# Attention's end in a two-block kernel: four outputs of the out projection in two parts

## The chip, the cores and the metric

One core of one Trainium2 chip runs the whole kernel. The metric is device time in microseconds of the core, and a kernel is judged by the median of its runs. The engines are TensorE (PE), VectorE (DVE), ScalarE (ACT), GpSimd (POOL) and SyncE (SP); each runs its own instructions in program order and waits on semaphores. PEld in the profile is TensorE's weight load, which overlaps its matmuls.

## What is computed

The input is 512 tokens of width 1024 in float32. A first block has two layers (stick-breaking attention, then an HGRN2 mixer, each followed by a squared-ReLU MLP), a second block two more. The change lies at the end of the attention of the first layer and at the start of the MLP behind it:

```python
def first_block(x, ...):
    for layer in range(DEPTH):
        h = rmsnorm(x, norm_gains[layer, 0])
        if layer % N_MIXERS == 0:
            x = x + stick_breaking_mixer(h, ...)   # ends with: return o @ w_o
        else:
            x = x + hgrn2_mixer(h, ...)
        h = rmsnorm(x, norm_gains[layer, 1])
        x = x + squared_relu_mlp(h, mlp_w1[layer], mlp_w2[layer])
    return x

def stick_breaking_attention(q, k, v):   # for each block of 128 queries
    log_stay = where(causal, log_sigmoid(-z), 0.0)
    log_between = cumsum(log_stay, axis=3, reverse=True) - log_stay
    weights = where(causal, exp(log_sigmoid(z) + log_between), 0.0)
    out = weights @ v
```

There are 16 heads of width 64. The out projection is 512 x 1024 by 1024 x 1024.

## The kernel before

**Layout.** Everything is kept transposed: x, h and the attention's output are [128 partitions, 8 blocks, 512 tokens], a block being 128 of the 1024 features. A product with a weight matrix is made of output tiles of 128 features. One output needs 8 weight blocks of 128 x 128 (k = 0 to 7), each against a 512 token block of the right input.

**Three matmuls a block.** For accuracy each operand is split into a high part (the value rounded to fp32r) and a low part (the rest). `gemm` (L234) issues, for the weight blocks it is given, first all high x high (L243), then high weights x low input (L247), then low weights x high input (L250). It waits for the high part of the weight tile at its head, for the low part only before L250. The last matmul of a tile raises `tile_used`.

**The weight stream.** Weights come as tiles of 8 blocks (512 KB) in one stream in the order of use. SyncE loads tile t into a ring of 4 raw buffers once the low part of tile t-3 is made (L1926). ScalarE makes the high part, `split_hi` (L215), into one of two buffers, which it may do only once tile t-2 is used. GpSimd makes the low part in four instructions of two blocks each, `split_lo` (L223), also into two buffers. In this stretch the tiles are called T (= T_ATT_O) to T+7 for the out projection, T+8 and on for the MLP. The outputs go by turns into two PSUM banks, `ps_g[0]` and `ps_g[1]`.

**The attention's pipeline.** Eight head pairs run through `pipelined` (L722), which in each step works on three of them in program order: g makes Q, K and V (three weight tiles), a computes scores and stick-breaking weights, b ends. The scores of a pair come in four units, for the query blocks 3, 2, 0, 1 in that order. A unit goes: scores on TensorE (L506); absolute value, exponential and logarithm on ScalarE (L580, L585, L590); add, two scans and subtract on VectorE (L656, L662, L664); exponential on ScalarE (L595); transposes on TensorE (L514); copies of the two heads by ScalarE (L600) and VectorE (L669). Two score units share their banks with the transposed weights, so a unit's scores wait for the copies of one before it. After the four units comes P.V (L524, 16 matmuls with 64-column weights into `ps_o`), then the high part by ScalarE (L605, `ohi`) and the low part by VectorE (L674, `olo`): these are block k of the out projection's input, k being the pair. V is turned by four transposes (L443) and a copy (L449).

**The drain.** In the step in which no g is left (a = pair 7, b = pair 6), `att_pe` gives TensorE parts of the out projection in the places of the QKV tiles: `out(0, 0, 3)`, `out(0, 3, 6)`, `out(1, 0, 3)`, `out(1, 3, 6)`, then block 6 of both. Their input blocks 0 to 6 are ready by then. The next step ends pair 7: its last transposes, P.V, ohi, olo. `out_begun_pe` then adds block 7 to outputs 0 and 1 and computes outputs 2 to 7 whole, 24 matmuls each:

```python
for d in range(2):
    gemm(pe, At(T + d), T + d, rhs, kts, False, True, ready, None, True)
for d in range(2, KT):
    gemm(pe, At(T + d), T + d, rhs, ALL, True, True, None, (x_ready, R + d - 1))
```

**Behind each output.** VectorE adds it to the residual x (`resid_dve`, L363, semaphore `x_ready`), ScalarE makes the high part of the next input h (L292) and the square of x (L382), VectorE the low part (L302) and the sum of squares (L374). `split_hi` of the tile after next stands ahead of each output's work on ScalarE (`out_act`).

**The MLP's start.** `ffn_pe` computes the first MLP tile T+8 in two halves of four blocks; between them stands `norm_pe` (L327), one product of a matrix of ones with the sum of squares (two passes), which needs all eight sums. The MLP's own norm factor is applied only at its end; ScalarE makes it from this sum ahead of the first relu (L309, L312; L857). A second MLP behind the other mixer runs the same code.

Of the kernel before, what the change touches and what calls it, by code (L numbers as in the profile page):

```python
# [8 lines left out]
P = 128  # L9
# [103 lines left out]
def build_program(nc, stream, ada_w, x_in, vecs_in, mats_in, lvmask_in, wgk_in, y_out):  # L113
    with ExitStack() as ctx:
# [119 lines left out]
        def gemm(pe, t, o, rhs, kts, first, last, waits=None, free=None, used=None, banks=None):  # L234
# [17 lines left out]
            if kts[-1][1] == KT - 1 if used is None else used:  # L252
                ins.then_inc(tile_used, 1)

        def h_rhs(k):
# [274 lines left out]


        def att_pe(pe, g, a, b):
            t = g.map(3, T_ATT) if g else None
            drain = a and not g

            def free(i):
                return (au_ready, t.of(1, i - 1)) if t.rep + i >= 2 else None

            def out(d, k0, k1):
                gemm(pe, At(T_ATT_O + d), T_ATT_O + d, a_rhs, ALL[k0:k1], k0 == 0, False,  # L540
                     lambda e, k, term: e.wait_ge(olo_ready, k + 1), (au_ready, 3 * PAIRS - 1 + d) if k0 == 0 else None)
# [24 lines left out]
            if g: gemm(pe, t + 2, t.rep, h_rhs, H1, True, False, None, free(2))  # L566
            if drain: out(0, 6, 7)
            if g: att_unit.pe_stat(pe, g.map(2, 1))
            if a: att_z(pe, a, 1)
            if drain: out(1, 6, 7)  # L570
            if a: att_wt(pe, a, 0)
            if g: gemm(pe, t + 2, t.rep, h_rhs, H2, False, True)
# [33 lines left out]

        def att_act(act, g, a, b):
            t = g.map(3, T_ATT) if g else None
            if a:
# [4 lines left out]
            if g: split_hi(act, t + 1)  # L614
            elif a: split_hi(act, At(T_ATT_O + 1))
            if b: att_first_act(act, b, 1)
# [76 lines left out]

        def att_dve(dve, g, a, b):
            if a: att_u_dve(dve, a, 2, vT_b)
            if b: att_second_dve(dve, b, 1)
# [18 lines left out]
        def att_pool(pool, g, a, b):  # L715
            t = g.map(3, T_ATT) if g else None
            if g:
                for i in range(3):
                    split_lo(pool, t + (i + 1))
            elif a: split_lo(pool, At(T_ATT_O + 1))  # L720

# [91 lines left out]
        def ffn_pe(pe, m, T, n, R, Q):  # L813
            for half in range(2):
                U = (2 * m + half) * FH
                for quarter in (2 * half, 2 * half + 1):
                    for j in quarter_loop(pe, m, quarter):
                        for k in range(4):
                            t, u = ffn_tile(m, T, quarter, j, k)
                            if quarter == 0 and j == 0 and k == 0:  # L820
                                pe.wait_ge(x_ready, R - 1)
                                gemm(pe, t, k, h_rhs, H1, True, False, h_waits(n), (relu_done, before(u)))
                                norm_pe(pe, n)
                                gemm(pe, t, k, h_rhs, H2, False, True, h_waits(n))
                            else:
# [1119 lines left out]
        def _(pe):  # L1945
            pipelined(pe, att_pe, PAIRS)
            out_begun_pe(pe, T_ATT_O, 0, lambda e, k, term: e.wait_ge(olo_ready, PAIRS), ALL[KT - 1:], a_rhs)
            ffn_pe(pe, 0, T_MLP0, 1, KT, 2 * KT)
# [10 lines left out]
        def _(act):  # L1959
# [9 lines left out]
            pipelined(act, att_act, PAIRS)  # L1969
            out_act(act, T_ATT_O, 0, KT, nxt=(1, GAIN[1]))  # L1970
            ffn_act(act, 0, T_MLP0, 1, KT, 2 * KT, (2, GAIN[2]))
# [10 lines left out]
        def _(dve):  # L1982
# [39 lines left out]
            pipelined(dve, att_dve, PAIRS)  # L2022
            out_dve(dve, T_ATT_O, 0, KT, nxt=(1, GAIN[1]))
            ffn_dve(dve, 0, T_MLP0, 1, KT, 2 * KT, (2, GAIN[2]))
# [14 lines left out]
        def _(pool):  # L2039
            split_lo(pool, At(0))  # L2040
            pipelined(pool, att_pool, PAIRS)
            out_pool(pool, T_ATT_O)
            ffn_pool(pool, 0, T_MLP0, 1, KT, 2 * KT)
# [8 lines left out]
def lay_out(np, a):  # L2052
# [6 lines left out]
    def ffn(w1, w2):  # L2059
        out = []  # L2060
        for half in range(2):
# [4 lines left out]
        return np.concatenate(out)  # L2066

    full = [P * d for d in range(KT)]
    stream = [tiles(a["sb_w_qkv"][0], [D_MODEL * m + P * p for p in range(PAIRS) for m in range(3)]),
              tiles(a["sb_w_o"][0], full), ffn(a["mlp_w1"][0], a["mlp_w2"][0]),  # L2070
              tiles(a["hg_w_in"][0], [D_MODEL * m + P * h for h in range(HG_HEADS) for m in (1, 2, 0, 3)]),
# [55 lines left out]
```

## Time and profile before

| | us |
|---|---|
| median of three runs (1850.20 to 1850.63) | 1850.24 |
| profiled execution, its own time | 1851.17 |
| its span, first to last instruction | 1849.4 |
| TensorE busy in the span | 1800.9 (97%) |
| last QKV tile's end to the first full out projection tile | 222.19 to 258.25 |
| from there to the first MLP tile T+8 | 258.25 to 291.24 |
| start of the second MLP tile, T+9 | 298.07 |

Times in the views are microseconds from the start of the span, "us" a duration; "mean ns" is that of one instruction. A row of the timeline may merge several instructions of one kind (x8), and the bracket is the time the engine sat idle before it and what ended that. Ends of matmuls are modelled and overlap the next start by 0.2 to 0.3 us, so distances between starts are the better measure of TensorE's work. PEclk is the granted clock, 1.00 for 2.4 GHz and 0.50 for 1.2 GHz.

### The profile page before, as it was taken

To read this page: it belongs to the slowest core of one execution; us is meant where nothing else is said; L and a number is where in the kernel's file an instruction comes from. 1 tells how busy PE (TensorE), PEld (TensorE's weight loads), DVE (VectorE), ACT (ScalarE), POOL (GpSimd) and SP (SyncE) were. 2 spreads that over 40 slices of the span, in tenths; PEclk is the share of its full clock that TensorE was granted. 3 is DMA by queue.
4 is the path that set the end of the run, shared out by engine and by line. 5 is a ranking of instruction groups with operands and counts; after the bars stand their busy time and mean duration, and the time that the engine had idled before them with its cause. 6 is when DMAs were issued, how large, how long until landed. Compare 5 with 4: busy or idle time off the path is not lost.

```text
span 1849.4 us, 25940 instructions
## 1 busy us (share of the span) xinstructions
PE 1800.9 (97%) x8406; PEld 1415.8 (77%) x8406; DVE 1029.0 (56%) x1659; ACT 891.5 (48%) x1384; POOL 890.1 (48%) x1072
## 2 busy tenths in 40 slices
PE   7999989999999999999899999999999999999999
PEld 5666658888888788888688888888776777776777
DVE  5677655621563377878666413643535565636562
ACT  6767744421333356666443312432456565455562
POOL 3343336755675533444217655766533336533343
PEclk9999989999999999999899999999999999999999
DMA  4111114432453222221145423533221222222212
GB/s 161 67 58 57 57 55 158 164 114 91 159 170 102 91 80 69 69 68 57 35 129 179 137 91 125 180 117 101 80 80 58 69 69 80 80 75 63 79 58 91
DMA packets 49659, 176.82 MB, mean 96 GB/s; under 512 B 5648, under 2 KB 5776, under 8 KB 49568
## 3 DMA queue, kind: packets, MB, share of 16 engines
q1 hardware_dynamic: 42368, 149.44, 25.5%
q10 hardware_dynamic: 7200, 26.22, 4.1%
q8 instruction: 50, 0.82, 0.2%
q14 instruction: 41, 0.34, 0.1%
HBM read 173.54 MB, written 2.10 MB: 95 GB/s over the span
## 4 chain that ended last, share of the span: by engine, by line
PE 81%; DVE 9%; ACT 4%; issue 3%; POOL 1%; DMA 0%; DVEq 0%; ACTq 0%; SPq 0%; POOLq 0%
PE ps_g L243 17%; PE ps_g L250 16%; PE ps_g L247 16%; PE ps_zt L243 6%; PE ps_zt L247 6%; PE ps_zt L250 6%; PE ps_s L1574 1%; PE ps_zt L514 1%; PE ps_zt L1623 1%; PE ps_zt L1001 1%; PE ps_o L524 1%; PE ps_o L1030 1%; PE ps_s L415 1%; PE ps_o L1638 1%; POOL w_lo L223 1%
## 5 line engine op out<-in xcount | busy, mean ns | idle before, releaser
L223 POOL TENSOR_TENSOR w_lo<-raw,w_hi 128x256 fp32r<-128x256 f32 x936 | 779.8, 863 | 791.9 <-ACT w_hi L215 790.6
L215 ACT ACTIVATE w_hi<-raw 128x1024 fp32r<-128x1024 f32 x274 | 288.8, 1054 | 376.7 <-PE ps_zt L250 247.0
L243 PE MATMUL ps_g<-h_hi,w_hi 128*128 128x512 f32 x1240 | 346.5, 409 | 10.1 <-ACT h_hi L292 8.6
L247 PE MATMUL ps_g<-h_lo,w_hi 128*128 128x512 f32 x1240 | 323.9, 391 | 1.0 <-DVE h_lo L302 1.0
L250 PE MATMUL ps_g<-h_hi,w_lo 128*128 128x512 f32 x1240 | 322.5, 390 | 0.7 <-POOL w_lo L223 0.4
L243 PEld LDWEIGHTS ps_g<-h_hi,w_hi 128*128 128x128 f32 x1240 | 224.4, 189 | 76.4 <-issue 23.6
L247 PEld LDWEIGHTS ps_g<-h_lo,w_hi 128*128 128x128 f32 x1240 | 233.3, 188 | 53.4 <-DVE h_lo L302 2.3
L250 PEld LDWEIGHTS ps_g<-h_hi,w_lo 128*128 128x128 f32 x1240 | 233.0, 188 | 51.2 <-POOL w_lo L223 1.2
L359 DVE TENSOR_TENSOR scr<-ps_zt,scr 128x512 f32<-128x512 f32 x32 | 22.1, 692 | 255.0 <-PE ps_zt L250 255.0
L857 ACT ACTIVATE scr<-ps_g 128x512 f32<-128x512 f32 x64 | 38.3, 599 | 193.2 <-PE ps_g L250 193.2
L243 PE MATMUL ps_zt<-a_hi,w_hi 128*128 128x512 f32 x512 | 128.6, 393 | 0.0
L247 PE MATMUL ps_zt<-a_lo,w_hi 128*128 128x512 f32 x512 | 127.4, 391 | 0.0
L250 PE MATMUL ps_zt<-a_hi,w_lo 128*128 128x512 f32 x512 | 126.9, 390 | 0.0
L243 PE MATMUL ps_g<-a_hi,w_hi 128*128 128x512 f32 x408 | 117.4, 412 | 6.7 <-DVE a_lo L1279 3.1
L243 PEld LDWEIGHTS ps_zt<-a_hi,w_hi 128*128 128x128 f32 x512 | 96.1, 188 | 21.8
L247 PEld LDWEIGHTS ps_zt<-a_lo,w_hi 128*128 128x128 f32 x512 | 96.1, 188 | 21.1
L250 PEld LDWEIGHTS ps_zt<-a_hi,w_lo 128*128 128x128 f32 x512 | 96.1, 188 | 20.6
L247 PE MATMUL ps_g<-a_lo,w_hi 128*128 128x512 f32 x408 | 108.7, 391 | 0.0
L250 PE MATMUL ps_g<-a_hi,w_lo 128*128 128x512 f32 x408 | 108.6, 391 | 0.0
L808 DVE TENSOR_TENSOR scr<-scr 128x1024 f32<-128x1024 f32 x48 | 69.9, 1456 | 59.4 <-DMA scr<-ada_weights 58.9
L243 PEld LDWEIGHTS ps_g<-a_hi,w_hi 128*128 128x128 f32 x408 | 73.5, 190 | 33.1 <-issue 15.0
L1318 POOL TENSOR_TENSOR scr<-scr 128x256 f32<-128x256 f32 x56 | 47.6, 849 | 92.7 <-DVE scr L1201 47.6
(211 smaller groups left out, 2402.4 us busy)
## 6 DMA issues: line engine op xcount, KB each, us to landing
raw<-weights SPq DMA_DIRECT2D x274, 512.0 KB, 3.5
scr<-ada_weights ACTq DMA_DIRECT2D x48, 512.0 KB, 4.2
x<-x_tiles SPq DMA_DIRECT2D x8, 256.0 KB, 5.7
y<-x SPq DMA_DIRECT2D x8, 256.0 KB, 3.2
scr<-csil_dram ACTq DMA_DIRECT2D x2, 512.0 KB, 5.7
lvmask<-level_masks SPq DMA_DIRECT2D x1, 960.0 KB, 9.3
mats<-squares SPq DMA_DIRECT2D x1, 448.0 KB, 7.0
vecs<-vectors SPq DMA_DIRECT2D x1, 95.5 KB, 2.0
```

What stands on the lines that cost most here:

```text
L215: nc.scalar.activation(w_hi[:, t.rep % 2], raw[:, raw_slot(t)], ACT.Copy).then_inc(whi_ready, 1)
L223: ins = nc.gpsimd.tensor_tensor(w_lo[:, t.rep % 2, ks], raw[:, raw_slot(t), ks], w_hi[:, t.rep % 2, ks].bitcast(F32), ALU.subtract)
L243: nc.tensor.matmul(bank[:], w_hi[:, t.rep % 2, kk], rhs(k)[0], start=(first and n == 0), stop=False)
L247: nc.tensor.matmul(bank[:], w_hi[:, t.rep % 2, kk], rhs(k)[1], start=False, stop=False)
L250: ins = nc.tensor.matmul(bank[:], w_lo[:, t.rep % 2, kk], rhs(k)[0], start=False, stop=(last and n == len(kts) - 1))
L359: nc.vector.tensor_tensor(tmp_x[0], bank, rstd_x, ALU.mult).then_inc(scaled, 1)
L415: nc.tensor.matmul(ps_s[:], mats[:, self.mat], self.sq, start=True, stop=True).then_inc(self.stat_ready, 1)
L514: ins = nc.tensor.transpose(z_bank[Z_SIDE[j]][:, h, P * i:P * i + P], e_b[j][:, h, P * i:P * i + P], mats[:, M_ID])
L524: ins = nc.tensor.matmul(ps_o[DH * h:DH * h + DH, P * i:SEQ], vtok[b.rep % 2][:, P * i + DH * h:P * i + DH * h + DH], wt_b[:, h, i, P * i: ...
L808: nc.vector.tensor_tensor(ada_b[slot], ada_b[slot], csil_row, ALU.mult).then_inc(ada_mul, 1)
L857: act.activation(r_b[k % 2], ps_g[k % 2][:], ACT.Relu).then_inc(relu_done, 1)
L1318: nc.gpsimd.tensor_tensor(packed(d[:, 0:HALF], w), queries(b, w), between(b, w, "odd"), ALU.subtract).then_inc(hd_ready, 1)
```

## The change

The drain has orders of its own on TensorE, ScalarE and VectorE (`att_drain_pe`, `att_drain_act`, `att_drain_dve`), which also end pair 7. Outputs 2, 3, 4 and 5 are computed in two parts: blocks 0 to 5 in the drain, whose sums VectorE adds to x at once (`cut_dve`), and blocks 6 and 7 behind it, added again (`cut_resid_dve`). Outputs 0 and 1 follow in the drain with blocks 0 to 6, and get block 7 behind it; outputs 6 and 7 are whole and last. The weight tiles are packed anew for this on the host: T, T+1 and T+2 hold the 24 blocks of the first parts, T+3 and T+4 outputs 0 and 1, T+5 the 8 blocks of the second parts, T+6 and T+7 outputs 6 and 7. In the drain TensorE no longer has outputs 0 and 1 in four pieces of three blocks but pieces of 6, 2, 4, 4, 2, 6, 3, 3, 6 and 1, 1 blocks. VectorE and ScalarE have their own order behind the drain as well (`cut_out_dve`, `cut_out_act`). In both MLPs the norm's matmul now stands behind the whole first tile, no longer between its halves.

```diff
+        CUT = {2: [(0, [(k, k) for k in range(6)])],
+               3: [(0, [(0, 6), (1, 7)]), (1, [(k, k - 2) for k in range(2, 6)])],
+               4: [(1, [(k, k + 4) for k in range(4)]), (2, [(4, 0), (5, 1)])],
+               5: [(2, [(k, k + 2) for k in range(6)])]}
+        WHOLE = {0: 3, 1: 4, 6: 6, 7: 7}
+        REST = 5
+        def cut_out_pe(pe, T, R, waits):
+            for d in range(2):
+                whole_pe(pe, T, d, [KT - 1], waits)
+            for d in CUT:
+                kts = [(KT - 2, 2 * d - 4), (KT - 1, 2 * d - 3)]
+                ins = gemm(pe, At(T + REST), d, a_rhs, kts, True, True, None, (x_ready, R + d - 1), d == 5)
+                if d < 5:
+                    ins.then_inc(part_done, 1)
+            for d in (6, 7):
+                gemm(pe, At(T + WHOLE[d]), d, a_rhs, ALL, True, True, None, (x_ready, R + d - 1))
+        def cut_dve(dve, T, d):
+            cut_done(dve, T, d, 0)
+            nc.vector.tensor_tensor(x[:, d], ps_g[d % 2][:], x[:, d], ALU.add).then_inc(part_read, 1)
+        def cut_out_dve(dve, T, Q, nxt):
+            for d in range(3):
+                cut_resid_dve(dve, T, d)
+            for d in range(3):
+                low(d)
+                cut_resid_dve(dve, T, d + 3)
+            for d in range(3, 6):
+                low(d)
+                sum_dve(dve, At(Q + d - 3))
+            for d in range(3, 6):
+                sum_dve(dve, At(Q + d))
+            for d in (6, 7):
+                cut_resid_dve(dve, T, d)
+                low(d)
+                sum_dve(dve, At(Q + d))
+        def cut_out_act(act, T, R, Q, nxt):
+            split_hi(act, At(T + REST))
+            high(0)
+            high(1)
+            split_hi(act, At(T + 6))
+            high(2)
+            square(0)
+            high(3)
+            square(1)
+            high(4)
+            split_hi(act, At(T + 7))
+            high(5)
+            for d in range(2, 6):
+                square(d)
+            split_hi(act, At(T + KT))
+            for d in (6, 7):
+                high(d)
+                square(d)
+        def att_drain_pe(pe, a, b):
+            att_z(pe, a, 3)
+            cut_pe(pe, T, 2, 0, ready, (au_ready, 3 * PAIRS - 1))
+            att_wt(pe, b, 1)
+            cut_pe(pe, T, 3, 0, ready, (au_ready, 3 * PAIRS))
+            att_z(pe, a, 2)
+            att_pv(pe, b)
+            cut_pe(pe, T, 3, 1, ready)
+            att_wt(pe, a, 3)
+            cut_pe(pe, T, 4, 0, ready)
+            att_z(pe, a, 0)
+            att_wt(pe, a, 2)
+            att_turn.pe(pe, a, vT_b, (au_ready, a.of(3, 3)), (olo_ready, a.v))
+            cut_pe(pe, T, 4, 1, ready)
+            att_z(pe, a, 1)
+            cut_pe(pe, T, 5, 0, ready)
+            att_wt(pe, a, 0)
+            whole_pe(pe, T, 0, [0, 1, 2], ready)
+            att_wt(pe, a, 1)
+            whole_pe(pe, T, 0, [3, 4, 5], ready)
+            att_pv(pe, a)
+            whole_pe(pe, T, 1, [0, 1, 2, 3, 4, 5], ready)
+            for d in range(2):
+                whole_pe(pe, T, d, [KT - 2], ready)
...
-            if drain: out(0, 0, 3)
...
-            if drain: out(0, 3, 6)
...
-            if drain: out(1, 0, 3)
...
-            if drain: out(1, 3, 6)
...
                                 gemm(pe, t, k, h_rhs, H1, True, False, h_waits(n), (relu_done, before(u)))
+                                gemm(pe, t, k, h_rhs, H2, False, True, h_waits(n))
                                 norm_pe(pe, n)
-                                gemm(pe, t, k, h_rhs, H2, False, True, h_waits(n))
```

The drain's order on the two other engines, each line one call (`w` is the exponential ahead of the transposes, `first` and `second` the copies of the two heads):

```
ScalarE: split T+1 | abs 3, exp 3 | w(b,1) | ln 3 | first(b,1) | split T+2 | abs 2, exp 2, ln 2 | w 3 | ohi(b)
         first 3 | w 2 | abs 0, exp 0 | first 2 | ln 0 | split T+3 | abs 1, exp 1 | w 0 | ln 1 | first 0
         split T+4 | w 1 | first 1 | ohi(a)
VectorE: V | second(b,1) | unit 3 | add 2 | unit 2 | second 3 | olo(b) | add 3 | second 2 | turn of V
         unit 0 | add 4 | unit 1 | second 0 | add 5 | second 1 | olo(a)
```

## Rows read from the trace of the kernel before

**Rows 1.** The page: busy time by engine, and the chain that ended last.

```profile
PE 1800.9 (97%) x8406; PEld 1415.8 (77%) x8406; DVE 1029.0 (56%) x1659; ACT 891.5 (48%) x1384; POOL 890.1 (48%) x1072
...
PE 81%; DVE 9%; ACT 4%; issue 3%; POOL 1%; DMA 0%; DVEq 0%; ACTq 0%; SPq 0%; POOLq 0%
```

**Rows 2.** Windows: length, then busy time (and count) of each engine, PEclk, DMA.

```profile
222.19:258.25 36.06, 26.31 (x125) 15.69 (x124) 21.49 (x30) 17.82 (x29) 4.65 (x4) 0.86 0.07 24
258.25:291.24 32.99, 32.99 (x144) 27.07 (x145) 17.81 (x20) 14.25 (x20) 26.36 (x28) 1.00 0.32 97
...
222.19:298.07 75.88, 65.87 (x295) 47.57 (x295) 41.82 (x54) 35.59 (x53) 33.81 (x36) 0.93 0.24 74
```

**Rows 3.** Timeline of TensorE: start, duration, engine, line, operation.

```profile
223.25 0.96 PE L243 MATMUL ps_g<-a_hi,w_hi 128*128 128x512 f32 x3
...
226.35 0.66 PE L514 MATMUL ps_zt<-mats,scr 128*128 128x128 f32 x4 [0.75 <-ACT scr L595]
...
229.86 2.37 PE L524 MATMUL ps_o<-scr 128*64 128x512 f32 x16
...
242.40 0.44 PE L514 MATMUL ps_zt<-mats,scr 128*128 128x128 f32 x2 [0.71 <-ACT scr L595]
248.43 1.11 PE L514 MATMUL ps_zt<-mats,scr 128*128 128x128 f32 x4 [5.60 <-ACT scr L595]
250.07 4.53 PE L524 MATMUL ps_o<-scr 128*64 128x512 f32 x16 [0.52 <-DVE scr L669]
256.11 0.47 PE L243 MATMUL ps_g<-a_hi,w_hi 128*128 128x512 f32 x1 [1.51 <-DVE a_lo L674]
...
258.25 2.11 PE L243 MATMUL ps_g<-a_hi,w_hi 128*128 128x512 f32 x8 [0.52 <-ACT w_hi L215]
```

**Rows 4.** Timeline of VectorE.

```profile
227.39 1.21 DVE L656 SCALAR_TENSOR_TENSOR scr<-ps_zt,scr 128x1024 f32<-128x1024 f32 x1
...
247.03 0.69 DVE L664 TENSOR_TENSOR scr<-ps_zt,scr 128x512 f32<-128x512 f32 x1
...
255.28 0.69 DVE L674 TENSOR_TENSOR a_lo<-ps_o,a_hi 128x512 fp32r<-128x512 f32 x1 [5.27 <-ACT a_hi L605]
```

**Rows 5.** Timeline of ScalarE.

```profile
232.98 1.06 ACT L595 ACTIVATE scr<-scr 128x1024 f32<-128x1024 f32 x1 [0.45 <-DVE scr L664]
...
257.14 1.06 ACT L215 ACTIVATE w_hi<-raw 128x1024 fp32r<-128x1024 f32 x1 [1.90 <-PE ps_g L250]
```

**Rows 6.** Timeline of GpSimd: the low parts of weight tiles.

```profile
228.27 4.65 POOL L223 TENSOR_TENSOR w_lo<-raw,w_hi 128x256 fp32r<-128x256 f32 x4 [8.27 <-ACT w_hi L215]
258.28 11.61 POOL L223 TENSOR_TENSOR w_lo<-raw,w_hi 128x256 fp32r<-128x256 f32 x12 [25.36 <-ACT w_hi L215]
...
294.44 2.81 POOL L223 TENSOR_TENSOR w_lo<-raw,w_hi 128x256 fp32r<-128x256 f32 x4 [3.48 <-ACT w_hi L215]
```

**Rows 7.** Windows around two falls of the granted clock.

```profile
244.50:245.00 0.50, 0.00 (x0) 0.00 (x0) 0.01 (x1) 0.46 (x1) 0.00 (x0) 0.96 0.00 0
...
920.00:922.00 2.00, 2.00 (x6) 1.10 (x6) 0.69 (x1) 1.06 (x2) 0.00 (x0) 0.70 0.00 0
```

**Rows 8.** Timeline of TensorE at the second fall.

```profile
919.91 0.47 PE L243 MATMUL ps_g<-a_hi,w_hi 128*128 128x512 f32 x1 [3.11 <-DVE a_lo L1279]
...
922.05 3.08 PE L243 MATMUL ps_g<-a_hi,w_hi 128*128 128x512 f32 x8
```

**Rows 9.** Groups by line and form, 222.19 to 298.07: count, busy, mean, idle before.

```profile
L374 DVE TENSOR_TENSOR acc<-acc,scr 128x512 f32<-128x512 f32 x8 | 9.3, 1158 | 0.0
L302 DVE SCALAR_TENSOR_TENSOR h_lo<-x,vecs,h_hi 128x512 fp32r<-128x512 f32 x8 | 6.6, 824 | 7.8 <-ACT h_hi L292 7.8
...
L363 DVE TENSOR_TENSOR x<-ps_g,x 128x512 f32<-128x512 f32 x8 | 5.5, 687 | 10.0 <-PE ps_g L250 10.0
```

**Rows 10.** Timeline of TensorE: the norm's matmuls in the two MLPs.

```profile
294.38 1.10 PE L327 MATMUL ps_s<-acc,mats 128*128 128x512 f32 x2 [0.26 <-issue]
...
958.94 1.10 PE L327 MATMUL ps_s<-acc,mats 128*128 128x512 f32 x2 [0.26 <-issue]
```

More of the change, by code:

```diff
@@ new lines, in cut_pe, with cut_done @@
+        def cut_pe(pe, T, d, piece, waits, read=None):
+            i, kts = CUT[d][piece]
+            ends = kts[-1][1] == KT - 1
+            last = piece == len(CUT[d]) - 1
+            ins = gemm(pe, At(T + i), d, a_rhs, kts, piece == 0, last, waits, cut_free(d, read) if piece == 0 else None, ends)
+            if last and not ends:
+                ins.then_inc(part_done, 1)
+        def cut_done(eng, T, d, n):
+            if d == 5:
+                eng.wait_ge(tile_used, T + CUT[d][-1][0] + 1 if n == 0 else T + REST + 1)
+            else:
+                eng.wait_ge(part_done, 3 * n + d - 1)
@@ new lines, in att_drain_act @@
+        def att_drain_act(act, a, b):
+            T = T_ATT_O
+            split_hi(act, At(T + 1))
+            att_abs_act(act, a, 3)
+            att_exp_act(act, a, 3)
+            att_wexp_act(act, b, 1)
+            att_ln_act(act, a, 3)
+            att_first_act(act, b, 1)
+            split_hi(act, At(T + 2))
+            att_abs_act(act, a, 2)
+            att_exp_act(act, a, 2)
+            att_ln_act(act, a, 2)
+            att_wexp_act(act, a, 3)
+            att_ohi_act(act, b)
+            att_first_act(act, a, 3)
+            att_wexp_act(act, a, 2)
+            att_abs_act(act, a, 0)
+            att_exp_act(act, a, 0)
+            att_first_act(act, a, 2)
+            att_ln_act(act, a, 0)
+            split_hi(act, At(T + 3))
+            att_abs_act(act, a, 1)
+            att_exp_act(act, a, 1)
+            att_wexp_act(act, a, 0)
+            att_ln_act(act, a, 1)
+            att_first_act(act, a, 0)
+            split_hi(act, At(T + 4))
+            att_wexp_act(act, a, 1)
+            att_first_act(act, a, 1)
+            att_ohi_act(act, a)
@@ L532, in att_pe @@
         def att_pe(pe, g, a, b):
+            if a and not g:
+                att_drain_pe(pe, a, b)
+            if not g:
+                return
             t = g.map(3, T_ATT) if g else None
-            drain = a and not g
             def free(i):
                 return (au_ready, t.of(1, i - 1)) if t.rep + i >= 2 else None
-            def out(d, k0, k1):
-                gemm(pe, At(T_ATT_O + d), T_ATT_O + d, a_rhs, ALL[k0:k1], k0 == 0, False,
-                     lambda e, k, term: e.wait_ge(olo_ready, k + 1), (au_ready, 3 * PAIRS - 1 + d) if k0 == 0 else None)
@@ L607, in att_act @@
         def att_act(act, g, a, b):
+            if a and not g:
+                att_drain_act(act, a, b)
+            if not g:
+                return
             t = g.map(3, T_ATT) if g else None
@@ L694, in att_dve @@
         def att_dve(dve, g, a, b):
+            if a and not g:
+                att_drain_dve(dve, a, b)
+            if not g:
+                return
             if a: att_u_dve(dve, a, 2, vT_b)
@@ L2041, in _ @@
             pipelined(pool, att_pool, PAIRS)
-            out_pool(pool, T_ATT_O)
+            for d in range(1, KT + 1):
+                split_lo(pool, At(T_ATT_O + d))
             ffn_pool(pool, 0, T_MLP0, 1, KT, 2 * KT)
@@ L2066, in ffn, with cut @@
         return np.concatenate(out)
+    def cut(w):
+        b = w.reshape(KT, P, KT, P).transpose(2, 0, 1, 3)
+        first = [b[d, k] for d in range(2, 6) for k in range(6)]
+        rest = [b[d, k] for d in range(2, 6) for k in (6, 7)]
+        whole = [[b[d, k] for k in range(KT)] for d in (0, 1, 6, 7)]
+        order = first + whole[0] + whole[1] + rest + whole[2] + whole[3]
+        return np.stack(order).reshape(KT, KT, P, P).transpose(0, 2, 1, 3).reshape(KT, P, KT * P)
     full = [P * d for d in range(KT)]
     stream = [tiles(a["sb_w_qkv"][0], [D_MODEL * m + P * p for p in range(PAIRS) for m in range(3)]),
-              tiles(a["sb_w_o"][0], full), ffn(a["mlp_w1"][0], a["mlp_w2"][0]),
+              cut(a["sb_w_o"][0]), ffn(a["mlp_w1"][0], a["mlp_w2"][0]),
               tiles(a["hg_w_in"][0], [D_MODEL * m + P * h for h in range(HG_HEADS) for m in (1, 2, 0, 3)]),
```

58 lines of the change are left out of this document (51 added, 7 removed).

## The prediction

> **What bounds the kernel now.** I read the page first: TensorE is busy 97% of the span, and the chain that ended last is TensorE for 81% of it, VectorE for 9% [rows 1]. So time can be won only where TensorE pauses or runs at the lower clock. The reader should look for stretches where both happen, and the attention's end is one, so I cut it into windows [rows 2]: 36.06 us from the last QKV tile's end to the first full out projection tile, then 32.99 us for 144 matmuls at full rate, about 0.227 us each once the two short hitches at their head are left out, and 75.88 us in all up to the second MLP tile (T+9, at 298.07). The timeline of TensorE shows the pauses [rows 3]: 0.75, 0.71, 5.60, 0.52, 1.51 and 0.52 us, nearly all before a transpose that waits for an exponential of ScalarE or before what follows the last of those. In the 5.60 us pause the granted clock fell from 2.4 to 1.2 GHz [rows 7], so that the last P·V took 4.53 us where the one before took 2.37, some 2.2 us more, and the transposes ahead of it 1.11 us where four others took 0.66. The last head pair is a chain of its own through VectorE's scans and ScalarE's exponentials [rows 4, 5]; TensorE runs out of other work at 242.84 and the chain ends at 255.97. Modelled ends hide another 0.2 to 0.3 us of each pause. Taken together: 75.88 us hold about 60.5 us of work at the full clock (64 blocks of 3 matmuls 43.5, the MLP's first tile 5.44, its norm matmul about 1.0, attention's own matmuls 10.5, by the distances between starts) and about 15.4 us of pauses and half clock. This is all that can be won here.
>
> **The change, part by part.** The number of matmuls stays the same. Before, 14 of 64 weight blocks run ahead of the last P·V's result being needed (6 of output 0, 6 of output 1, then block 6 of both). Now it is 38: 24 blocks of outputs 2 to 5 are added, 24 x 3 x 0.227 = 16.3 us of work moved from behind the chain into it. That is more than there is to fill, so the question is what it delays. I walk the new program orders with the durations of the rows; a wait between engines costs about 0.04 us.
>
> *Into the chain.* Six blocks (4.08 us) of output 2 now stand ahead of the transposes of pair 6's last unit, where three stood. They start at 227.33, not 226.35, and VectorE's long unit of the last pair with them: its first op 228.37 for 227.39 [rows 4], the exponential behind it 233.97 for 232.98 [rows 5]. VectorE then does the first of four new additions (0.6 us each, of the kind of L363 [rows 9]) ahead of the next unit, so the exponential behind that one comes at 238.27, 1.6 us later than before. TensorE meanwhile does blocks 0, 1 of output 3, scores, P·V from 229.95, blocks 2 to 5 of output 3 (234.97), transposes from 235.08 (0.1 us lost), blocks 0 to 3 of output 4, and waits 0.3 us for VectorE's copy before the next scores at 238.90. Transposes, V's turn, blocks 4, 5 of output 4, the last scores at 241.83 (240.09 before), then output 5's six blocks to 246.55. ScalarE ends that unit's logarithm at 244.68, VectorE's unit runs 244.70 to 247.42 (it ended at 247.72 before [rows 4]): the last unit is not later, because before it also waited in ScalarE's queue behind other work. One split of a weight tile (1.06 us [rows 5]) stands before its exponential, which starts at 248.17. The transposes follow at 248.84 behind three blocks of output 0, and P·V at 251.29 behind three more, at the full clock: 2.3 us. Its split into high and low took 1.4 us before, from 254.60 to 255.97 [rows 3, 4], and ends at 255.05, under six blocks of output 1 and two more, which last until 259.03. So the chain costs TensorE about 0.5 us in all, and 259.03 is where 256.11 was, with 24 blocks more behind it.
>
> The four additions and the GpSimd splits lie under this: tile T+3's low part may take 4.65 us beside scans [rows 6], from 242.05 to 246.7, and is wanted at 248.1; if that cover went it would cost its excess alone. The weight loads wait for GpSimd two or more tiles ahead on SyncE's queue and have over 8 us in each case. ScalarE's split of T+1, moved ahead of its first absolute value, delays that by 0.4 us, which VectorE's own start at 228.37 hides.
>
> *Behind the chain.* Tile T+5 (blocks 6, 7 of outputs 2 to 5) can be split only when tile T+3 is used, by its last block. In the rows the first last-block starts at 256.11, the split at 257.14 and the next tile's matmuls at 258.25 [rows 3, 5]. That makes 261.09 from 259.03 now, a pause of 0.7 us. Then TensorE has only 4 matmuls (0.9 us) before it needs the low part, where it had 16 (3.6 us). GpSimd needs 2.81 us for a tile when VectorE is quiet and 3.87 when VectorE runs L302 and L374 (12 quarter tiles in 11.61) [rows 6]. VectorE does only residual additions there, so I take 2.81: 261.12 to 263.93, a second pause of 1.9 us; at 3.87 it is 1.06 us more. The Trainium skill ("SBUF — State Buffer", on the port pair shared by GpSimd and VectorE) says that a VectorE instruction with two SBUF inputs collides with GpSimd's reads, and one with a single SBUF input does not; a residual addition reads one operand from PSUM, so by the rule the price is the lower one too. The rows agree in that L302 and L374, with two SBUF inputs, are what ran in the slow case.
>
> From 263.97 the four short outputs follow in 1.36 us each; the two banks must be read between them, and VectorE puts a low part (0.82 on average [rows 9], up to 1.3 by my estimate beside GpSimd) after each 0.69 us residual: 0.3 us lost, output 6 at 268.85, output 7 at 274.29, its end at 279.73. Before it ended at 291.24. T+8's split stands behind four squares on ScalarE, which follow VectorE's sums (1.16 us each on average while GpSimd works [rows 9]). I get 277.3 to 278.35 for the split, and 281.2 to 282.2 for GpSimd's part, wanted at 281.5: 0.3 us. Output 7's residual now follows output 6's sum at about 281.8 instead of at once, its low part is ready at 284.05, and the second half of T+8 wants it at 284.1: just hidden.
>
> *The norm behind the MLP's first tile.* Its matmul pair costs TensorE 0.5 and 0.4 us as before, but without the pause ahead [rows 10]: T+9 starts at 286.45. In the second MLP the same swap gives 0.4 us (by the gap before 958.94 [rows 10], longer than its printed 0.26 by the modelled ends). ScalarE's first relu comes about 2 us later in its tile; the split for T+10 then ends near 290.2 and GpSimd's part by 294.9 at 4.7 us, wanted at 295.5.
>
> *Sum.* 298.07 − 286.45 = 11.6, plus 0.4 = 12.0 us. Read the other way: 15.4 us of pauses and half clock become 3.8 us. The profiled execution took 1851.17 us with a span of 1849.4; I expect a span of 1837.4. The median of 1850.24 less 12.0 gives 1838.2 us. The most that rows allow: with no loss but T+5's 2.6 us the gain is 13.2, 1837.0 us.
>
> **The rivals.**
> 1. *Half clock behind the chain.* The two pauses of 0.7 and 1.9 us with 0.9 us of work between are like the 0.7 us pause, short work and idleness before the clock fell at about 245.0; but pauses of 1.51 and 0.52 us at 256 to 258 left it full. A second case in the trace gives the price: after a pause of 3.1 us the clock fell at about 920.9, one microsecond after work began again, and eight matmuls took 3.08 us [rows 7, 8] for about 1.8: 1.7 us lost over that low stretch. Gain 10.3, 1840.0 us. 2 in 10. The Trainium skill ("TensorE: Matmul & The Clock Gate", Part 1) says that the clock is granted by recent activity and that lack of it throttles; by that a change that adds a 2.6 us lull right after the chain could give back that amount, and the trace's two falls agree in kind.
> 2. *The splits are later than walked.* T+5's low part at 3.87 us (1.06), T+8's at 4.65 beginning a microsecond late (2.0), the late residual of output 7 up to 1 us. These three have one cause, VectorE and GpSimd slowing each other. Gain 8 to 10: about 1841.2 us. For it: L374 takes 1.16 us on average in this stretch. Against: the order of VectorE leaves it quiet at T+5. 2 in 10.
> 3. *The chain does not overlap.* If the moved blocks lengthen the last pair's chain by their own time, 16.3 us, nothing is won in it, and the thin cover behind (0.7 + 1.9 + 0.3 + 0.3, against 0.52 and some 0.3 before) costs about 2 us: 1852.5 us, slower. It decides once the chain's end at 255.97 moves out by more than some 12 us; the 18 matmuls queued ahead of three of its steps would each have to be paid in full, whereas the walk shows each under VectorE's units (5.56 us for the long one, from 227.39 to 232.95 [rows 4, 5]) or ScalarE's work. 4 in 100.
> 4. *Something in the drain absorbs most of it*, such as a bank wait of output 3 or 5 that holds the in-order TensorE ahead of the last scores: by what a fill of the 5.60 us pause alone is worth, below 3.7 us gain. 4 in 100.
>
> **How the numbers follow.** The forecast case has 5 in 10 and its own range is 1837.0 to 1839.6. Rivals 1 and 2 fill the other side up to 12.0 − 1.7 − 2.6 = 7.7 us gain, 1842.5 us. Range 1837.0 to 1842.5. About 0.2% (3.7 us) is what a measurement of this kernel can tell from no change: faster 0.92, same 0.04, slower 0.04.
>
> **What would show it.** In the profile after: no TensorE pause above 0.5 us between 222 and 259; the last P·V at about 251.3 taking 2.4 us; granted clock 1.00 up to 259; two pauses, about 0.7 and 1.9 us, at 260 to 264, the first ended by ScalarE's split, the second by GpSimd; output 7 ending near 279.7; T+9 near 286.5; and the distance of everything behind it unchanged but for 0.4 us at the second MLP. I would be wrong if TensorE idles before the transposes of unit 1 as before, if the clock is down in 264 to 270, or if a later stretch gives the time back.

## The result and the profile after

The changed kernel takes 1840.66 us (median of five runs, 1839.65 to 1841.63) against 1850.24. The ratio is 0.9949, with a 95% interval of 0.9939 to 0.9959: by that ratio 9.4 us faster (7.6 to 11.3), by the two medians 9.6. Its first profiled execution was its fastest run: 1839.65 us, span 1837.8, mean clock 0.998. Profile against profile the gain is 1849.4 − 1837.8 = 11.6 us.

The page, as in [rows 1]: TensorE's busy time and the chain.

```profile
PE 1797.3 (98%) x8406; PEld 1413.8 (77%) x8406; DVE 1034.5 (56%) x1663; ACT 891.6 (49%) x1384; POOL 885.8 (48%) x1072
...
PE 81%; DVE 9%; ACT 4%; issue 4%; POOL 2%; DMA 0%; DVEq 0%; ACTq 0%; SPq 0%; POOLq 0%
```

Windows, as in [rows 2]: the same 36.06 us, and the stretch from the last pair's first scores (222.03, before at 222.19) to the third MLP tile, T+10. It starts at 292.70 now; before, T+9 started at 298.07 [rows 2] and T+10 5.44 us later, at 303.51.

```profile
222.19:258.25 36.06, 36.06 (x184) 26.01 (x185) 23.76 (x33) 19.15 (x29) 12.98 (x16) 1.00 0.22 65
222.03:292.70 70.67, 68.14 (x319) 51.03 (x319) 46.24 (x61) 37.60 (x56) 31.59 (x39) 1.00 0.29 92
```

In the first window TensorE was busy for 26.31 us at a clock of 0.86 before; now it is busy for all of it at 1.00. Its timeline, as in [rows 3]:

```profile
223.09 1.65 PE L243 MATMUL ps_g<-a_hi,w_hi 128*128 128x512 f32 x6
224.58 1.54 PE L247 MATMUL ps_g<-a_lo,w_hi 128*128 128x512 f32 x6
...
227.32 0.60 PE L515 MATMUL ps_zt<-mats,scr 128*128 128x128 f32 x4
...
230.08 2.38 PE L525 MATMUL ps_o<-scr 128*64 128x512 f32 x16
...
238.94 0.49 PE L507 MATMUL ps_zt<-scr 64*128 64x128 f32 x4
...
246.84 0.38 PE L515 MATMUL ps_zt<-mats,scr 128*128 128x128 f32 x2
...
249.15 0.60 PE L515 MATMUL ps_zt<-mats,scr 128*128 128x128 f32 x4
...
251.78 2.37 PE L525 MATMUL ps_o<-scr 128*64 128x512 f32 x16
...
259.66 0.39 PE L243 MATMUL ps_g<-a_hi,w_hi 128*128 128x512 f32 x1
...
261.71 0.73 PE L243 MATMUL ps_g<-a_hi,w_hi 128*128 128x512 f32 x2 [0.53 <-ACT w_hi L215]
...
264.59 0.73 PE L250 MATMUL ps_g<-a_hi,w_lo 128*128 128x512 f32 x2 [1.68 <-POOL w_lo L223]
...
269.30 2.09 PE L243 MATMUL ps_g<-a_hi,w_hi 128*128 128x512 f32 x8
...
282.60 1.20 PE L250 MATMUL ps_g<-h_hi,w_lo 128*128 128x512 f32 x4 [0.31 <-POOL w_lo L223]
...
286.36 1.02 PE L328 MATMUL ps_s<-acc,mats 128*128 128x512 f32 x2
286.81 2.42 PE L243 MATMUL ps_g<-h_hi,w_hi 128*128 128x512 f32 x8
```

The transposes at 246.84 and 249.15 stand where 242.40 and 248.43 stood in [rows 3], now without a pause ahead of them; the last P.V takes 2.37 us for 4.53. The two pauses that are left come behind the chain: 0.53 us until ScalarE's high part of T+5, 1.68 us until GpSimd's low part. T+8 waits once more (0.31). The norm's matmul at 286.36 has no pause ahead of it [rows 10]. VectorE, ScalarE and GpSimd, as in [rows 4 to 6]:

```profile
228.30 1.21 DVE L844 SCALAR_TENSOR_TENSOR scr<-ps_zt,scr 128x1024 f32<-128x1024 f32 x1
...
246.91 0.69 DVE L852 TENSOR_TENSOR scr<-ps_zt,scr 128x512 f32<-128x512 f32 x1
...
254.83 0.69 DVE L862 TENSOR_TENSOR a_lo<-ps_o,a_hi 128x512 fp32r<-128x512 f32 x1 [4.62 <-ACT a_hi L790]
```

```profile
233.67 1.06 ACT L780 ACTIVATE scr<-scr 128x1024 f32<-128x1024 f32 x1 [0.76 <-DVE scr L852]
...
260.60 1.06 ACT L215 ACTIVATE w_hi<-raw 128x1024 fp32r<-128x1024 f32 x1 [5.80 <-PE ps_g L250]
```

```profile
242.10 2.94 POOL L223 TENSOR_TENSOR w_lo<-raw,w_hi 128x256 fp32r<-128x256 f32 x4 [7.79 <-ACT w_hi L215]
...
261.74 6.27 POOL L223 TENSOR_TENSOR w_lo<-raw,w_hi 128x256 fp32r<-128x256 f32 x8 [10.35 <-ACT w_hi L215]
```

The last unit ends at 247.60 (247.72 before), the chain at 255.52 (255.97). ScalarE splits T+5 at 260.60; GpSimd makes two tiles' low parts in 6.27 us, T+5's in 2.81 of them.

Behind T+10 two places differ lastingly: the start of the second MLP is 0.49 us shorter (first tile to third: 12.27 us before, from 955.80 to 968.07; 11.78 now, from 944.73 to 956.51), and the stretch ahead of it 0.26 us. So the 11.6 us are 10.81 up to T+10 (303.51 − 292.70), 0.26, 0.49 and 0.04. The last number is a difference of two chance events in the second block, where the kernels are alike: before, the scores at 1501.29 came after a pause of 1.37 us where the changed kernel's had 0.76; the changed kernel's at 1758.93 came after 1.38 where those before had 0.77.

### The profile page after: what moved, and what is told of

It is laid out like the page before. It is cut to its first block, busy times and chain, and to the rows that moved or that the text cites. A ratio compares the mean times of both kernels' runs of the same rounds, so it can differ in the third digit from the quotient of the medians.

```text
span 1837.8 us, 25961 instructions
## 1 busy us (share of the span) xinstructions
PE 1797.3 (98%) x8406; PEld 1413.8 (77%) x8406; DVE 1034.5 (56%) x1663; ACT 891.6 (49%) x1384; POOL 885.8 (48%) x1072
## 4 chain that ended last, share of the span: by engine, by line
PE 81%; DVE 9%; ACT 4%; issue 4%; POOL 2%; DMA 0%; DVEq 0%; ACTq 0%; SPq 0%; POOLq 0%
PE ps_g L243 17%; PE ps_g L250 16%; PE ps_g L247 16%; PE ps_zt L243 6%; PE ps_zt L247 6%; PE ps_zt L250 6%; PE ps_s L1765 1%; POOL w_lo L223 1%; PE ps_zt L515 1%; PE ps_zt L1814 1%; PE ps_zt L1192 1%; PE ps_o L525 1%; PE ps_o L1221 1%; PE ps_s L416 1%; PE ps_o L1829 1%
```

## The experiments

Each was run beside the kernel before. The medians of that kernel on the chips used lay between 1849.47 and 1850.35 (one chip has a single run of it, 1849.45), so a time is read against the one beside it.

**The changed kernel again.** No edit.

> The changed kernel once more, with five timed runs and a profile of its own. Its first profile showed one pause of 0.5 us and one of 1.7 us on TensorE at 261 to 265 with the clock at 1.00, in the fastest of its five runs (mean clock 0.998; the others 0.996 to 0.997 and about 1 us slower). Theory A: in some executions those two pauses let the clock fall at about 264, for 1 to 2 us; then the runs spread over some 2 us, by their clock, and a profile of a slow one shows PEclk below 1.00 between 262 and 268. Theory B: what varies is the stretch of the other mixer's end (about 885 to 915), which both kernels have; then PEclk is 1.00 there every time. Median 1840.5, gain 9.5 to 10.5 us by either.

Measured: 1841.32 us (1841.04 to 1842.65) beside 1850.35, ratio 0.9953 (0.9939 to 0.9966); the gain of 9.0 us is a little under the 9.5 to 10.5 expected. TensorE's timeline of this execution:

```profile
261.93 0.72 PE L243 MATMUL ps_g<-a_hi,w_hi 128*128 128x512 f32 x2 [0.53 <-ACT w_hi L215]
...
264.81 0.86 PE L250 MATMUL ps_g<-a_hi,w_lo 128*128 128x512 f32 x2 [1.69 <-POOL w_lo L223]
265.46 1.05 PE L243 MATMUL ps_g<-a_hi,w_hi 128*128 128x512 f32 x2
266.32 1.05 PE L247 MATMUL ps_g<-a_lo,w_hi 128*128 128x512 f32 x2
267.17 1.05 PE L250 MATMUL ps_g<-a_hi,w_lo 128*128 128x512 f32 x2
...
268.79 0.63 PE L247 MATMUL ps_g<-a_lo,w_hi 128*128 128x512 f32 x2
```

The pauses are the same, but a row of two matmuls then took 1.05 us instead of 0.62: the clock was at 0.50 from about 265.3 to 268.7. The full-speed rows return at 268.79. From T+5's low part to output 6 it was 6.29 us (264.81 to 271.10), in the first profile 4.71 (264.59 to 269.30): the fall cost 1.6 us there. Of that 0.2 us came back by T+10, which started 1.4 us later counted from the first scores. So theory A's fall exists. A third profile was taken of the same code, and a fourth comes below:

> The changed kernel's third profile. Of its ten timed runs one took 1839.65 (its first profile, no fall of the clock behind the chain) and most 1841.0 to 1841.6 (as in the second, with a fall at 265). So this one most likely shows PEclk at 0.50 between about 265 and 268 and 1841.3; without the fall, 1839.7.

Measured: 1841.18 us, without a fall behind the chain.

**The pause filled.** Eight matmuls that nobody reads, ahead of the wait for the low part:

```diff
...
+            if filled[0]:
+                filled[0] = False
+                for i in range(8):
+                    nc.tensor.matmul(ps_o[:], w_hi[:, t.rep % 2, 0], rhs(kts[0][0])[0], start=True, stop=True)
             pe.wait_ge(wlo_ready, t.of(1, 1))
...
+                if d == 2:
+                    filled[0] = True
```

> The changed kernel with 8 matmuls whose result nobody reads, into the bank of P.V, in the 1.7 us pause before T+5's low part. They take 1.8 us, as long as the pause between starts, so they cost at most 0.1 us of TensorE's time and can win nothing but the clock. Theory A (the pauses trip the clock at about 264 in most executions; it fell in the second profile of the changed kernel, at 0.50 from about 265.3 to 268.3, and cost 1.6 us there): PEclk stays 1.00 there in the profile, the times come down to those of the changed kernel's fastest run, 1839.7 to 1840.2. Theory B (the fall at 264 is rare): 1841.0, as the changed kernel.

Measured: 1839.46 us (1839.17 to 1842.21), ratio 0.9950 (0.9937 to 0.9964), on another chip than the changed kernel. So both were timed side by side:

> The changed kernel beside the one with its pause filled, on one chip. Three profiles of it so far: the clock fell behind the chain (265 to 268) in one, at a cost of 1.6 us; in another it stayed up there but was down for longer in the other mixer's end (888 to 904), at about the same cost; in the first neither. If the fall behind the chain happens in about a third of the executions or more, this kernel's mean is at least 0.5 us above the filled one's. If what varies is mainly the other mixer's end, the two agree within 0.3 us.

> The same 8 unread matmuls in the pause as in pause_filled, now timed on the chip on which the changed kernel is timed. It took 1839.2 to 1839.7 in four of five runs and 1842.2 in one, but on another chip than the changed kernel, where the kernel before was 0.9 us faster too. 0.5 us or more below the changed kernel if its clock falls behind the chain in a third of the executions, level with it otherwise; its own spread, up to 3 us, can only come from elsewhere.

Measured: 1840.08 us (1839.70 to 1840.47) and 1839.13 us (1838.74 to 1839.33). The filled kernel is 0.95 us faster and the two ranges don't meet. But the trace puts that elsewhere: in this execution of the changed kernel the clock stayed at 1.00 behind the chain. The eight matmuls in the filled one, after which the low part follows without a pause:

```profile
262.51 2.00 PE L253 MATMUL ps_o<-a_hi,w_hi 128*128 128x512 f32 x8
```

The end of the other mixer (HGRN2, in the second layer) as a window (the seventh group is PEclk), first in the changed kernel's first profile, then in this one, then in the filled one:

```profile
885.00:930.00 45.00, 37.74 (x175) 30.76 (x174) 25.79 (x45) 19.54 (x33) 6.59 (x8) 0.92 0.13 40
```

```profile
885.00:930.00 45.00, 37.74 (x164) 31.20 (x163) 25.11 (x44) 17.97 (x31) 6.59 (x8) 0.85 0.11 36
```

```profile
885.00:930.00 45.00, 37.73 (x173) 30.75 (x172) 25.80 (x45) 19.57 (x33) 6.59 (x8) 0.92 0.13 42
```

0.85 against 0.92 over 45 us. So of four profiles of the changed kernel one had the fall behind the chain, two (this one and the 1841.18 us one) a longer stretch of half clock at the other mixer's end, and the fastest neither. Against the first profile those two reached the second MLP's norm 1.6 and 2.1 us later (951.77 and 952.24 for 950.17). Both theories hold in part.

The mean clocks of the timed runs say more than the few profiles: 0.998 in nine of the filled kernel's ten runs, in one of the changed kernel's sixteen (0.996 or 0.997 in the others). So the higher clock does go with the filled pause. Which stretch it comes from isn't shown, since the filled kernel's two profiles lack both the fall behind the chain and the longer one.

**A second profile of the kernel before.** No edit.

> The kernel before once more, for a second profile of it. The first one took 1851.17 us where the median of all its runs is about 1850.0, at a mean clock of 0.994 where most of its runs show 0.996. If the chip's clock does not fall at the same place each time, this one shows less time at half clock in the 5.6 us pause and the P.V behind it (244 to 256), or in the other mixer's end (900 to 925), and is 1 us faster by just that: 1850.0, clock 0.996. If the first profile's falls are always there, it shows the same windows and 1851.

Measured: 1850.65 us, span 1848.8, clock 0.995, between the two cases expected. In the drain it shows the same fall (0.66 over 243 to 258 in both), in the other mixer's end 0.92 for 0.89. So the loss at half clock in the drain was there in both profiles of this kernel. The shorter stretch at the other mixer's end is worth only 0.14 us: the second MLP's norm starts at 958.80 for 958.94 [rows 10]. The rest of the 0.6 us comes at full clock, at the scores of 1501.29 named above (1500.59 here, after 0.77 us).

**Less work in the drain.** Output 5's blocks 0 to 4 are left out:

```diff
-               5: [(2, [(k, k + 2) for k in range(6)])]}
+               5: [(2, [(5, 7)])]}
```

> The changed kernel without blocks 0 to 4 of output 5: 15 matmuls, 3.4 us of TensorE's work left out of the middle of the drain (that output is then incomplete). Theory: the drain is in balance, TensorE's work and the last pair's chain through VectorE and ScalarE take about equally long, so only 0.8 us is won (the last exponential at 247.6 instead of 248.4, no longer behind the split of T+4) and a pause of some 2.5 us appears ahead of the last transposes: 1840.2, up to 1.7 more if that pause trips the clock. Rival: TensorE's work alone sets the drain, then all 3.4 us are won: 1837.6.

Measured: 1841.69 us (1841.14 to 1842.81); output 5 is incomplete in this kernel. In TensorE's timeline the last transposes come 26.85 us behind the first scores; in the changed kernel it was 27.12:

```profile
222.48 1.13 PE L507 MATMUL ps_zt<-scr 64*128 64x512 f32 x4
...
244.82 0.44 PE L515 MATMUL ps_zt<-mats,scr 128*128 128x128 f32 x2 [0.78 <-ACT scr L780]
...
249.33 0.66 PE L515 MATMUL ps_zt<-mats,scr 128*128 128x128 f32 x4 [2.00 <-ACT scr L780]
```

3.4 us of work were taken out and 0.3 won; pauses of 0.78 and 2.00 us took its place, and in this execution the clock fell at about 265 as well. The rival (TensorE's work sets the drain) is refuted: here the chain is the longer one. Of the 0.8 us expected the chain itself took 0.6 back: the last unit's two scans took 1.84 us (from 246.05) for 1.27 in the changed kernel (from 245.60). GpSimd's low part of T+4 ran beside them, from 246.60; in the changed kernel it came behind them, at 248.56.

**The additions three times.** Two extra additions into scratch before each of the four:

```diff
+            for i in range(2):
+                nc.vector.tensor_tensor(tmp_x[i], ps_g[d % 2][:], x[:, d], ALU.add)
```

> The changed kernel with each of the four additions in the drain done three times (the two extra ones go to a scratch buffer): 8 more VectorE instructions of 0.6 us. Walk: the first pair delays the next scores by 1.2 us; the others run into idle time of VectorE (0.55 us ahead of a copy, 0.72 us ahead of the last unit) before they delay the last unit by some 2.3 us, of which 1.5 reach TensorE at the last transposes. Expected 1.5 us slower than the changed kernel, 1842.5. If the additions were hidden altogether: 1841. If each lay on the path: 4.8 us, 1845.8.

Measured: 1840.91 us (1840.13 to 1842.43), not the 1842.5 expected. The times can't tell it from the changed kernel; the trace can:

```profile
221.92 1.13 PE L507 MATMUL ps_zt<-scr 64*128 64x512 f32 x4
...
239.68 0.49 PE L507 MATMUL ps_zt<-scr 64*128 64x128 f32 x4 [0.77 <-DVE scr L859]
...
250.28 0.66 PE L515 MATMUL ps_zt<-mats,scr 128*128 128x128 f32 x4 [0.25 <-ACT scr L782]
```

The scores wait 0.77 us for VectorE's copy, and the last transposes come 28.36 us behind the first scores, 1.24 later than in the changed kernel, for 4.8 us of added VectorE work. That is near the 1.5 us walked. The real additions are thus nearly, not wholly, hidden.

**The old blocks in other places.** The kernel before, output 1's seven blocks moved ahead of the last transposes:

```diff
-            if drain: out(1, 0, 3)
...
-            if drain: out(1, 3, 6)
...
-            if drain: out(1, 6, 7)
...
+            if b and not a:
+                out(1, 0, 6)
+                out(1, 6, 7)
             if b: att_wt(pe, b, 1)
```

> The kernel before with the same 14 blocks in the drain, but output 1's seven moved from the middle of it to ahead of the last transposes, where TensorE idled for 5.6 us. Nothing is added. If the gain of the change comes from the amount of work that lies under the chain, the sum of the pauses stays: the earlier ones grow by what the last one loses. What can be won is the clock: the 5.6 us pause in which it fell shrinks to about 1, so the 2.6 us lost at half clock come back: 1847.6. If place alone mattered, 1845 or less; if the clock falls elsewhere instead, 1850.

Measured: ratio 1.0000 (0.9991 to 1.0009), median 1849.93 (1849.01 to 1854.51) beside 1850.35. TensorE's timeline:

```profile
234.14 1.09 PE L514 MATMUL ps_zt<-mats,scr 128*128 128x128 f32 x8 [1.86 <-ACT scr L595]
237.62 1.54 PE L514 MATMUL ps_zt<-mats,scr 128*128 128x128 f32 x6 [2.40 <-ACT scr L595]
...
239.82 1.11 PE L443 MATMUL ps_o<-mats,scr 128*128 128x128 f32 x4
...
243.80 0.44 PE L514 MATMUL ps_zt<-mats,scr 128*128 128x128 f32 x2 [1.46 <-ACT scr L595]
...
249.85 0.66 PE L514 MATMUL ps_zt<-mats,scr 128*128 128x128 f32 x4 [0.82 <-ACT scr L595]
251.02 2.37 PE L524 MATMUL ps_o<-scr 128*64 128x512 f32 x16 [0.52 <-DVE scr L669]
...
257.05 2.10 PE L243 MATMUL ps_g<-a_hi,w_hi 128*128 128x512 f32 x8 [0.52 <-ACT w_hi L215]
```

The pause of 5.60 us is gone, and in its place stand 1.86, 2.40, 1.46 and 0.82 us. All printed pauses from the first scores to T+2 (output 2's tile) add up to 9.8 us here and in the kernel before: they moved and did not shrink. The last P.V ran at full clock, but the clock fell at about 237.6 instead: the transposes at 237.62 and 239.82 are slow (1.54 us for 0.87, 1.11 for 0.66). 1.2 us came back up to T+2 (257.05 for 258.25), from the clock, but the timed median did not move measurably (in this profile the other mixer's end had the longer stretch of half clock, 0.85 over 885 to 930). Place alone won nothing that the times show.

**The norm's matmul alone.** The kernel before with the swap in `ffn_pe`:

```diff
                                 gemm(pe, t, k, h_rhs, H1, True, False, h_waits(n), (relu_done, before(u)))
+                                gemm(pe, t, k, h_rhs, H2, False, True, h_waits(n))
                                 norm_pe(pe, n)
-                                gemm(pe, t, k, h_rhs, H2, False, True, h_waits(n))
```

> The kernel before with one part of the change alone: the norm's matmul behind the MLP's whole first tile, in both MLPs. My walk: 0.4 us in each MLP, 0.8 together, 1849.4. Rival: the later norm delays the first relu by 2 us, the split of the tile after next with it, and TensorE waits for the low part: gain 0, or slower by up to 1 us.

Measured: ratio 0.9998 (0.9989 to 1.0007), which holds 0.8 us and nothing. In the trace T+8 to T+10 takes 11.79 us for 12.27, and so do the same tiles of the second MLP (955.46 to 967.25):

```profile
291.32 1.07 PE L243 MATMUL ps_g<-h_hi,w_hi 128*128 128x512 f32 x4
...
296.76 1.02 PE L327 MATMUL ps_s<-acc,mats 128*128 128x512 f32 x2
297.22 2.42 PE L243 MATMUL ps_g<-h_hi,w_hi 128*128 128x512 f32 x8
...
303.11 1.98 PE L243 MATMUL ps_g<-h_hi,w_hi 128*128 128x512 f32 x8
```

So by its trace the swap is about 1.0 us of the 11.6 in the two MLPs; the rest is the drain and what follows it.

**Output 0 ended early.** Output 1's work now covers the split of T+5:

```diff
             att_pv(pe, a)
-            whole_pe(pe, T, 1, [0, 1, 2, 3, 4, 5], ready)
-            for d in range(2):
-                whole_pe(pe, T, d, [KT - 2], ready)
+            whole_pe(pe, T, 1, [0, 1, 2], ready)
+            whole_pe(pe, T, 0, [6, 7], ready)
+            whole_pe(pe, T, 1, [3, 4, 5, 6, 7], ready)
...
-            for d in range(2):
-                whole_pe(pe, T, d, [KT - 1], waits)
```

> The changed kernel with output 0 ended early: blocks 0 to 2 of output 1, then blocks 6 and 7 of output 0, then blocks 3 to 7 of output 1. Tile T+3 is used about 3 us sooner, so the high and the low part of T+5 are there when TensorE comes to it. Both pauses behind the chain should go: 0.7 and 1.9 us between starts, less the short hitch of a start, gain 2.2 to 2.6 us on the changed kernel, 1838.2. If theory A holds (the pauses trip the clock in some runs) the gain is up to 1.5 us more and the runs spread less. Rival: output 0's end now waits for the last low part of the chain; then a new pause ahead of its block 7 takes back up to 1 us.

Measured: 1838.31 us (1837.41 to 1840.55), ratio 0.9939 (0.9926 to 0.9953), span 1835.6, 2.2 us under the changed kernel's first.

```profile
260.95 0.62 PE L243 MATMUL ps_g<-a_hi,w_hi 128*128 128x512 f32 x2
...
261.86 0.70 PE L250 MATMUL ps_g<-a_hi,w_lo 128*128 128x512 f32 x2
...
266.55 2.08 PE L243 MATMUL ps_g<-a_hi,w_hi 128*128 128x512 f32 x8
...
280.50 1.21 PE L250 MATMUL ps_g<-h_hi,w_lo 128*128 128x512 f32 x4 [1.00 <-POOL w_lo L223]
```

T+5's first matmuls (260.95) and low part (261.86) follow without a pause; T+6 starts 2.7 us sooner than in the changed kernel. But ScalarE's split of T+8, behind the squares of outputs 2 to 5, now comes late for it, and 1.00 us is lost at 280.50.

**On top of it, T+8's split and the residuals moved.**

```diff
-            for d in range(2, 6):
-                square(d)
+            square(2)
+            square(3)
             split_hi(act, At(T + KT))
+            square(4)
+            square(5)
...
             for d in (6, 7):
                 cut_resid_dve(dve, T, d)
+            for d in (6, 7):
                 low(d)
+            for d in (6, 7):
                 sum_dve(dve, At(Q + d))
```

> Output 0 ended early (2.2 us by the two profiles), and with it two changes against the pause of 1.0 us at T+8's low part that this brought: ScalarE splits T+8 after the third square, not after the fifth, and VectorE adds outputs 6 and 7 one after the other before their low parts and sums. The pause before T+8's low part goes; 1.1 us more than ending output 0 early alone: a span of 1834.5 against 1835.6 in profiles with the same falls of the clock, median 1837.2. Rival: the second half of T+8 now waits for the low part of output 7's residual instead, and 0.5 to 1 us is lost again.

Measured: 1837.21 us (1836.49 to 1839.86) beside 1849.47, ratio 0.9936 (0.9923 to 0.9950): the lowest median of all, but its ratio can't be told from the 0.9939 of the kernel above, and its interval overlaps with that of the changed kernel. The trace shows the step: T+9 starts at 283.88 where it started at 284.76, after a new short wait of 0.21 us for a residual:

```profile
277.85 1.20 PE L243 MATMUL ps_g<-h_hi,w_hi 128*128 128x512 f32 x4 [0.21 <-DVE x L588]
...
279.80 1.07 PE L250 MATMUL ps_g<-h_hi,w_lo 128*128 128x512 f32 x4
...
283.88 2.42 PE L243 MATMUL ps_g<-h_hi,w_hi 128*128 128x512 f32 x8
```

That is 0.9 us of the 1.1 expected. The profiled execution itself took 1839.05 us (span 1837.2), for it had the long stretch of half clock at the other mixer's end (0.85 over 885 to 930). It has neither pause behind the chain, so those pauses are not needed for the longer stretch.

## Why the prediction was right, and where it was off

**The range and the sign held; the gain was 2.4 us smaller than forecast** (9.6 us for 12.0, 1840.66 for 1838.2). Of that, 0.5 us is the walk (11.5 us between the two profiled executions) and 1.9 us the choice of executions. The median lies outside the forecast case's own range, 1837.0 to 1839.6: it fell into the part of the range that was there for rivals 1 and 2. The mechanism of the drain was right; that the time came out near rival 1's 1840.0 is in part chance, since its fall is in one of four profiles.

*The chain.* Its steps came 0.2 to 0.5 us later than walked: the last unit 247.60 (walked 247.42), the last exponential 248.38 (248.17), the last transposes 249.15 (248.84), P.V 251.78 (251.29), its low part's end 255.52 (255.05). Output 0's block 7 began at 259.66, not 259.03, though the trace started 0.16 us earlier, so "The chain costs TensorE about 0.5 us in all" was about 0.8 us short. It wasn't waits: of the 0.1 and 0.3 us walked ahead of transposes and scores, the distances between starts show 0.0 and 0.1. What grew is TensorE itself: 18 matmuls as a group took 4.2 us between starts (223.09 to 227.32), not 4.08; 0.13 of that at their head (223.09 to 224.58 is 1.49 for six).

*Behind the chain.* The term "0.7 and 1.9 us" measured 0.53 and 1.68 us as printed; between starts, less the work between them, the pauses are 0.7 (260.34 + 0.68 to 261.71) and 1.9 (2.88 from 261.71 to 264.59, less 0.99 for the four matmuls); from block 7's start to the low part it was 4.93 us, walked as 4.94. GpSimd took 2.81 us for T+5 and 3.7 for T+8 (from 278.82), and no wait for output 7's residual shows, so rival 2 did not occur. T+8's wait was 0.48 us between starts, not 0.3.

*The norm.* "0.4 us" in the second MLP measured 0.49; the late relu had cost nothing.

*The sum.* 286.45 for T+9 answers to 287.26, since 0.45 us of the norm's cost fall into T+9 itself (286.81): 0.8 us late. Against that, the stretch up to the second MLP gave 0.26 us, the second MLP 0.09 more than walked, and the rest 0.04. So 12.0 became 11.6.

*The step that was mis-sized* is the last: "The median of 1850.24 less 12.0". The profiled execution of before took 0.9 us more than its median, that of the changed kernel 1.0 us less. The sum was right to 0.5 us for these two and 2 us too large for the medians. Rival 1 named one cause at the right place and price (walked 1.7 us, measured 1.6, 265.3 to 268.7), but it showed in one of four profiles. The other, half clock at the other mixer's end for longer in two of four (0.85 for 0.92 in the window), stood in no rival. Nor did the chance pause of 0.6 us in the second block, which the first profile of before has at 1501.29 and the second one lacks. The Trainium skill ("TensorE: Matmul & The Clock Gate", Part 1) says that the number of matmuls which one and the same kernel runs at the low clock at its start differs from run to run. The traces show a spread of that kind for falls in mid-kernel: the same code, the same two pauses, a fall in one execution and none in three.

*Rivals 3 and 4* did not occur: the chain ended at 255.52, 0.45 us sooner than before and not 12 us later, and TensorE had no pause in the drain. The two experiments on the work say why. Less of it won 0.3 of 3.4 us, and the old blocks in new places won nothing measurable: what paid was the added work under a chain of fixed length, which the changed drain just fills. Not settled: which executions get which fall, and why the filled pause went with a higher mean clock in nine of ten runs.

## What to carry to other kernels

A chain of fixed length on the other engines is paid once; count the independent work that can lie under it, and move that much in from behind, no more. Then look at what the moved work covered before: here a tile's low part, made under 16 matmuls, came to stand under 4. And a sum made against one profiled execution is good only to the spread between executions: put its distance to the median into the range when the gain is of the same order.

## What was not expected of the hardware

The clock fell to 0.50 after two pauses of 0.53 and 1.69 us with 1.0 us of matmuls between, and in some executions only: in one of four profiles of the changed kernel, in the one with less work in the drain and not in the one with more additions, whose pauses there are the same. It also fell in the pause of 5.60 us, in both profiles of the kernel before, and 0.8 us after work began again behind one of 3.11 us [rows 7, 8]. The stretch of half clock at the other mixer's end had two lengths, with 0.92 or 0.85 over 885 to 930, in kernels that are alike there; the eight added matmuls went with the shorter one in both their profiles, but so did two of four profiles without them, so that they shorten it is not shown. And a run of these matmuls costs about 0.1 us at its head when one of another form stood ahead: the six from 223.09, behind the scores, took 1.49 us up to 224.58, where six of 0.227 make 1.36.
